# One product of 512 adjacent columns in place of two of 256 in the up projections of two MLPs, with the halves added afterwards

## The reference, cut to what matters

```python
def sq_relu_mlp(h, w1, w2):            # block 1, w1: 1024 x 4096, w2: 4096 x 1024
    return jnp.square(jax.nn.relu(h @ w1)) @ w2
x = x + gt2[..., None, :] * sq_relu_mlp(modulate(rms_norm(x, norm2), sh2, sc2), w_mlp1, w_mlp2)
...
def sqrelu_mlp(xn, w1, w2):            # block 2, the same sizes
    return jnp.square(jax.nn.relu(xn @ w1)) @ w2
h = h + sqrelu_mlp(rmsnorm(h, norm_mlp[i]), mlp_w1[i], mlp_w2[i])
```

## Time and profile before

| | |
|---|---|
| median of three executions | 941.5 us (940.83 to 945.18) |
| the profiled execution: its time | 941.33 us |
| the profiled execution: span from first to last instruction | 939.5 us |
| its mean granted TensorE clock, as a share of full speed | 0.996 |
| instructions | 14931 |
| PE, DVE, ACT busy, of the span | 97%, 66%, 51% |
| matmuls of 256 columns in `product` | 3 x 896 |
| matmuls of 512 columns in `product` | 3 x 592 |

### The profile page before, as it was taken

How to read it: one execution, slowest core, us unless ns; L and a number is a source line. 1 busy time by engine, 2 the same in 40 slices (tenths; PEclk the granted TensorE clock), 3 DMA queues, 4 the chain that set the end, 5 groups by cost and what they waited for, 6 DMA issues and landing times.

```text
span 939.5 us, 14931 instructions
## 1 busy us (share of the span) xinstructions
PE 913.5 (97%) x5552; PEld 789.9 (84%) x5552; DVE 621.5 (66%) x976; ACT 481.8 (51%) x760; POOL 9.7 (1%) x21
## 2 busy tenths in 40 slices
PE   7999999999999999999999999999999999999994
PEld 2778888897789999879999998887888999999883
DVE  1748779769777878765555557655777745555575
ACT  4645455555656565545444444443655544444464
POOL 0200000000000000000000000000000000000000
PEclk9999999999999999999999999999999999999998
DMA  9935212325346767635555557353434765555531
GB/s 361 333 117 201 70 66 90 109 93 176 118 140 220 266 213 259 203 129 185 180 180 181 195 194 261 106 165 128 135 113 146 268 225 179 179 183 194 194 100 45
DMA packets 45347, 162.02 MB, mean 172 GB/s; under 512 B 5616, under 2 KB 5760, under 8 KB 45297
## 3 DMA queue, kind: packets, MB, share of 16 engines
q1 hardware_dynamic: 42896, 155.73, 48.7%
q0 software_dynamic: 1264, 3.89, 1.4%
q10 hardware_dynamic: 1136, 1.70, 0.5%
HBM read 160.25 MB, written 1.05 MB: 172 GB/s over the span
## 4 chain that ended last, share of the span: by engine, by line
PE 83%; DVE 8%; DMA 3%; ACT 3%; issue 1%; SPq 0%; ACTq 0%; DVEq 0%
PE bank L671 71%; DVE w_lo L1613 3%; DMA raw<-in_early 2%; PE bank L828 2%; PE bank L911 1%; DMA arena<-in_early 1%; PE bank L1097 1%; PE bank L818 1%; PE bank L926 1%; PE bank L931 1%; PE bank L835 1%; PE bank L785 1%; DMA raw<-in_stream 1%; ACT w_hi L1194 1%; PE bank L849 1%
## 5 line engine op out<-in xcount | busy, mean ns | idle before, releaser
L1613 DVE TENSOR_TENSOR w_lo<-raw,w_hi 128x1024 fp32r<-128x1024 f32 x246 | 289.8, 1219 | 168.4 <-ACT w_hi L1194 167.9
L1194 ACT ACTIVATE w_hi<-raw 128x1024 fp32r<-128x1024 f32 x246 | 246.1, 1050 | 188.7 <-PE bank L671 169.2
L671 PE MATMUL bank<-act_lo,w_hi 128*128 128x256 f32 x896 | 257.9, 288 | 1.7 <-DVE act_lo L1613 0.9
L671 PE MATMUL bank<-act_hi,w_lo 128*128 128x256 f32 x896 | 253.5, 283 | 0.0
L671 PE MATMUL bank<-act_hi,w_hi 128*128 128x256 f32 x896 | 253.4, 283 | 0.0
L671 PE MATMUL bank<-w_hi,act_lo 128*128 128x512 f32 x592 | 238.5, 403 | 0.0
L671 PE MATMUL bank<-w_hi,act_hi 128*128 128x512 f32 x592 | 231.1, 390 | 0.0
L671 PE MATMUL bank<-w_lo,act_hi 128*128 128x512 f32 x592 | 230.7, 390 | 0.0
L671 PEld LDWEIGHTS bank<-act_lo,w_hi 128*128 128x128 f32 x896 | 171.7, 192 | 5.8 <-DVE act_lo L1613 2.1
L671 PEld LDWEIGHTS bank<-act_hi,w_hi 128*128 128x128 f32 x896 | 171.8, 192 | 1.4 <-issue 0.7
L671 PEld LDWEIGHTS bank<-act_hi,w_lo 128*128 128x128 f32 x896 | 171.7, 192 | 0.0
(11 more groups left out here) (243 smaller groups left out, 785.8 us busy)
## 6 DMA issues: line engine op xcount, KB each, us to landing
raw<-in_stream SPq DMA_DIRECT2D x278, 512.0 KB, 4.4
arena<-in_early SPq DMA_DIRECT2D x12, 512.0 KB, 10.0
raw<-in_early SPq DMA_DIRECT2D x4, 512.0 KB, 15.4
res<-in_x ACTq DMA_DIRECT2D x1, 1024.0 KB, 8.9
arena<-in_ctx SPq DMA_DIRECT2D x1, 1024.0 KB, 14.5
res<-in_x POOLq DMA_DIRECT2D x1, 1024.0 KB, 8.2
arena<-in_norm_final POOLq DMA_DIRECT2D x1, 512.0 KB, 4.4
arena<-in_ple_b POOLq DMA_DIRECT2D x1, 512.0 KB, 5.2
```

The source lines that it names most:

```text
L671: last = pe.matmul(o, left, right, start=start and m == 0, stop=stop and m == 2, skip_group_check=shared)
L1194: return act.activation(o, i, ACT.Copy)
L1613: return dve.tensor_tensor(o, x, hi.bitcast(F32), ALU.subtract)
```

## The change

The activations are laid out as high left, low left, high right, low right, 256 columns each, in one tensor `act`, so that 512 adjacent columns hold an MLP's input as high part and low part. `act_hi` and `act_lo` become views of it, and the right half begins at column `RIGHT` = 512.

An up tile's block and chunk now takes two matmuls in place of three: high weights by the 512 columns (high and low), and low weights by the 256 high columns, added to the left half of the same bank. A block fills a whole bank, and the sum of its two halves is the result. Every tile uses banks 4 to 7, one per block ("b"'s tile 0 uses 4, 5 and two of the banks 0 to 3), so block b of a tile waits until block b of the tile before has been read. ACT copies each block's right half out of PSUM (four of 128 x 256 per tile in place of two relus of 128 x 512); DVE adds the left half (four of 128 x 256 that are new) and then makes the squared relu as max(x, 0) * x in one instruction per two blocks; ACT then writes the rounded copy of that in place of the square. PE's `ada_fin` waits until block 0 of tile 7 has been read.

```diff
+RIGHT = 2 * T
+BLK0 = {"a": 0, "b": 4 * FF_STEPS}
+FIRST_BANKS = {"a": (4, 5, 6, 7), "b": (4, 5, GROUP_AT["wmo0", 0] % 4, GROUP_AT["wmo0", 1] % 4)}
...
-        act_hi = sb("act_hi", [P, KC, 2 * T], F32R)
-        act_lo = sb("act_lo", [P, KC, 2 * T], F32R)
+        act = sb("act", [P, KC, 4 * T], F32R)
+        act_hi, act_lo = act[:, :, 0:3 * T], act[:, :, T:4 * T]
...
+            def up_chunk(bank, ts, k, col):
+
+                cols_ = slice(col, col + P)
+                pe.matmul(bank[:, :], w_hi[:, ts, k, cols_], act[:, k, 0:2 * T], start=(k == 0), stop=False,
+                          skip_group_check=True)
+                return pe.matmul(bank[:, 0:T], w_lo[:, ts, k, cols_], act_hi[:, k, 0:T], start=False, stop=(k == KC - 1),
+                                 skip_group_check=True)
...
@@ first_up
-                    for g in range(2):
-                        for b in range(2):
...
+                    for b in range(4):
+                        if half == 0 and b >= 2:
+                            if tag == "b":
+                                pe.wait_ge(evac_dve, EVAC["wmo0", b - 2][1])
+                            else:
+                                wait_block(pe, name, b)
+                        for k in range(4 * half, 4 * half + 4):
+                            if b == 0 and k % 2 == 0:
+                                wait_cut(pe, UNIT[tag + "u0", k // 2])
+                            last = up_chunk(psum[FIRST_BANKS[tag][b]], ts, k, b * P)
                         if half == 1:
                             last.then_inc(hid_done, 1)
-                        elif g == 0 and tag == "b":
+                        elif b == 1 and tag == "b":
                             turn(name, (2, 3))
@@ up
-                for g in range(2):
-                    if not (isinstance(i, int) and i < 2):
-                        pe.wait_ge(relu_done, 2 * i + (UP0[tag] + g - 3))
...
+                for b in range(4):
+                    pe.wait_ge(add_done, 4 * i + (BLK0[tag] + b - 3))
+                    for k in range(KC):
+                        if b == 0 and k % 2 == 0:
+                            wait_cut(pe, 8 * i + (first + k // 2))
+                        last = up_chunk(psum[4 + b], ts, k, b * P)
                     last.then_inc(hid_done, 1)
@@ mlp of PE
                 if tag == "a":
+                    pe.wait_ge(add_done, BLK0[tag] + 4 * FF_STEPS - 3)
                     ada_fin(psum[4], 11).then_inc(gt_done, 1)
@@ hidden of ACT
+                banks = FIRST_BANKS[tag] if isinstance(i, int) and i == 0 else (4, 5, 6, 7)
+                for b in range(4):
+                    act.wait_ge(hid_done, 4 * i + (BLK0[tag] + b + 1))
+                    if b % 2 == 0 and not (isinstance(i, int) and i == 0 and tag == "a"):
+                        act.wait_ge(hsq_done, 2 * i + (UP0[tag] + b // 2 - 1))
+                    act.activation(hid_r[:, b // 2, b % 2 * T:(b % 2 + 1) * T], psum[banks[b]][:, T:2 * T],
+                                   ACT.Copy).then_inc(cross_done, 1)
                 for g in range(2):
-                    act.activation(hid_r[:, g], psum[4 + 2 * c + g][:, :], ACT.Relu).then_inc(relu_done, 1)
...
-                    act.activation(act_hi[:, 4 * c + 2 * g:4 * c + 2 * g + 2, T:2 * T],
-                                   hid_r[:, g].rearrange("p (b t) -> p b t", b=2), ACT.Square).then_inc(hhi_done, 1)
+                    hi_part(act_hi[:, 4 * c + 2 * g:4 * c + 2 * g + 2, RIGHT:RIGHT + T],
+                            hid_h[:, g].rearrange("p (b t) -> p b t", b=2)).then_inc(hhi_done, 1)
@@ hidden of DVE
                 for g in range(2):
-                    dve.wait_ge(relu_done, 2 * i + (UP0[tag] + g + 1))
-                    dve.tensor_tensor(hid_h[:, g], hid_r[:, g], hid_r[:, g], ALU.mult).then_inc(hsq_done, 1)
+                    for b in (2 * g, 2 * g + 1):
+                        dve.wait_ge(cross_done, 4 * i + (BLK0[tag] + b + 1))
+                        cross = hid_r[:, g, b % 2 * T:(b % 2 + 1) * T]
+                        dve.tensor_tensor(cross, psum[banks[b]][:, 0:T], cross, ALU.add).then_inc(add_done, 1)
+                    dve.wait_ge(add_done, 4 * i + (BLK0[tag] + 2 * g + 2))
+                    dve.scalar_tensor_tensor(out=hid_h[:, g], in0=hid_r[:, g], scalar=0.0, in1=hid_r[:, g], op0=ALU.max,
+                                             op1=ALU.mult).then_inc(hsq_done, 1)
```

More of the change, by code:

```diff
@@ L731, in mm @@
                 elif kind == "lr":
+                    both = act[:, :, :].rearrange("p k (h v t) -> p v k h t", h=2, v=2)
                     for k in range(KC):
-                        last = product(o[0:2 * RANK, :], (lr_w[0][:, k], lr_w[1][:, k]), acts(k), slice(0, 2 * T),
-                                       slice(0, 2 * RANK), k == 0, k == KC - 1, feature_major=True)
+                        last = product(o[0:2 * RANK, :].rearrange("p (h t) -> p h t", h=2), (lr_w[0][:, k], lr_w[1][:, k]),
+                                       (both[:, 0, k], both[:, 1, k]), slice(0, 2), slice(0, 2 * RANK), k == 0,
+                                       k == KC - 1, feature_major=True)
                 elif kind == "p":
@@ L744, in mm @@
                             wait_chunks(k)
-                        last = product(o[:, :], chunk(n, k), acts(k), slice(base + which * P, base + which * P + P),
-                                       slice(0, NC), k == 0, k == KC - 1)
+                        at = base + which * P if which < TT else RIGHT + (which - TT) * P
+                        last = product(o[:, :], chunk(n, k), acts(k), slice(at, at + P), slice(0, NC), k == 0,
+                                       k == KC - 1)
                 elif n in ("gk", "mq"):
@@ L1314, in turn @@
                 i, y = TURN_AT[name], turn_y
-                half = T if name == "n1" else 0
+                half = RIGHT if name == "n1" else 0
                 for b in quarters:
```

53 lines of the change are left out of this document (17 added, 36 removed).

## The result

| | before, same chip | after |
|---|---|---|
| median | 941.37 us (10 runs, 940.76 to 945.18) | 943.51 us (10 runs, 941.59 to 945.02) |
| profiled execution, its span | 941.33, 939.5 us | 942.63, 940.8 us |
| mean granted clock of the profiled execution | 0.996 | 0.995 |

The ratio is 1.0023, with an interval of 1.0014 to 1.0031: 2.1 us slower where 2.0 us faster than the profiled execution was forecast. The time lies inside the predicted range and within 0.5% of before, but on the other side of it.

The account below looks back on a forecast made before the run. The prediction took PE, busy for 97% of the span, to bound the kernel. Gains of 1.8 us in "a" and 0.2 in "b" took 941.33 us to 939.3, with a range of 936.0 to 944.0.

Parts of the forecast that it names:

- The pair: In up tiles, one 512- and one 256-column matmul cost 347 ns, not 360: 0.41 us less per tile.
- Rivals 1: Up tiles: the weight load is hidden wholly, 340 ns a pair, 0.64 us a tile, 936.1 us; chance 0.13.
- Rival 3: Up tiles: the pair gains nothing, costing the 360 ns of three; 4.1 us slower, 945.4 us; chance 0.07.
- Of DMAs nothing is added or moved: Whole kernel: each DMA is issued when its unit is cut, and cuts stay tied to the ends of tiles.
- Loop: Middle tiles: `hidden` takes DVE 2.0 us more, but all new waits cost nothing, with 0.5 to 4 us in hand.
- Start of "a": Up 1 of the first MLP needs tile 0's banks, read by 419.1; PE arrives at 422.3, no wait.
- End of "a": First MLP's end: tile 7's 0.41 us is lost, down 7 starts 2.0 us later and "mq" moves by 1.1.
- Start of "b": Second MLP: up 1 waits for DVE's first add of tile 0; PE idle 3.1 us, up 1 ends 2.0 late.
- End of "b": Second MLP's end: `hidden` ends at 886.5 where PE asks at 886.22, costing 0.3 us.
- Rival 2: At three edges the waits don't come and all 16 tiles count: 6.6 us, 934.7 us; chance 0.06.
- rival 4: The clock falls in the new idle stretch before up 1 of "b": 11.1 us more, 950.4 us; chance 0.08.
- The sum: Whole kernel: 1.8 us gained in "a" and 0.2 in "b", 2.0 in all, giving 939.3 us.

Follow-up runs that it names:

- e2: The changed kernel with each block's long products (512 columns) all before its short ones (256): 942.46 us, ratio 1.0015.
- e8: The changed kernel with the short product added to the right half of the bank instead of the left: 942.0 us, one run.
- e1: The changed kernel with GpSimd's wait before the loads of norm_final and ple_b put back to its old place: 943.57 us, ratio 1.0024.
- e9: The changed kernel with an extra unused max-and-square on DVE, twice per loop tile, 1.2 us together: 944.69 us, ratio 1.0033.
- e11: e6 with down 7's first part waiting for the low parts by halves, its first two chunks needing only the first: 937.34 us, ratio 0.9958.
- e6: The changed kernel with the edits of e1, e2 and e3 together: 938.73 us, ratio 0.9977.
- e12: e11 with one useless matmul behind `ada_fin` at the end of the first MLP: 937.13 us, ratio 0.9956.
- e10: The changed kernel with useless matmuls in both new idle stretches, three before up 1 of "b", two at the end of "a": 942.41 us, ratio 1.0014.
- e3: The changed kernel with up tiles 1 to 7 of the second MLP using banks in the order 6, 7, 4, 5: 939.42 us, ratio 0.9984.
- e4: The changed kernel with six useless fp32 matmuls of 512 columns in front of up 1 of the second MLP: 944.01 us, ratio 1.0039.

## Why the prediction was wrong, step by step

**The pair was mis-sized. This is the step that failed.** "So a pair costs 227 + 120 = 347 ns" took both transitions from the edges of tiles, and both are right there and in e2's first block of eight. In the loop a pair costs 353. That is half the gain: 0.22 us a tile and not 0.41, some 2.5 us less over the 13 tiles that the sum counted. Why the loop has 353 is open: e8 rules out the half of the bank, e2 shows that grouping brings it to 348, and tiles 0 and 1 of "a" in e1 show that the same order can cost 347. The bounds of 340 and 360 held it; my own narrower range of 344 to 352 did not. Rivals 1 and 3 fall with it. (Rival 3's 2.7 us in "b" should have been 2.4, 731.7 + 11.5 against 740.80, and its time 945.1; nothing else hangs on that.)

By an estimate from the gap that the Trainium skill gives (TensorE: Matmul & The Clock Gate, Back-to-back issue gap), a pair takes 325 ns and three products of 256 take 328. e2 shows 226 and 120 where it has 216 and 109, so the forecast was right to go by the rows.

**"Of DMAs nothing is added or moved" was wrong.** I counted the DMAs of SyncE's ring, and not the wait of GpSimd on a semaphore whose count the change doubles. Price, by e1: 0.42 us of stall against the profiled execution of after, but nothing against that of e8, whose loads are as early.

**The waits came where they were forecast, though not all for the reasons given.** Loop: covered, shown by e9. Start of "a": no wait; up 0 itself started 0.36 earlier, outside the change's reach. End of "a": from up 7's start to "mq" 36.37 us became 37.66 (557.36 and 555.64 to the earlier trace rows and 593.30), 1.3 longer where 1.1 was forecast. That is near by luck, since two steps were wrong the opposite way: DVE's cuts for "mq" were to move by 1.1 and moved by 0.59, and "PE's own four parts, two transposes and 11 us fit into that" was false, since DVE waits 0.61 us for PE's third part. e11, where PE starts down 7 earlier, has "mq" 1.0 earlier. Start of "b": idle 3.12 us where 3.1 was forecast; down 0 was to start at 742.8 and started at 742.96. On the scale of the stage, which began 0.39 earlier, that is 0.55 worse: 0.4 by DVE's later cuts, beside the early loads, and 0.1 by up 1's pace. That the idle time agrees to 0.02 us is luck too: on that scale DVE's first add and PE's arrival (729.03, for 728.6 forecast) both came 0.4 late. End of "b": 0.3, as forecast (e11 gets 0.3 back there: from the start of down 6 to the last part of down 7 PE takes 19.86 us, in e6 20.16). Rival 2 falls.

**The clock** was rival 4, with the right mechanism and the wrong size and place. The price put on it was an up tile at half clock, 11.1 us; in e1 it is 2.9 us, since the clock is back before the tile is half through, and in e6 and e9 1.6 and 1.7. It does not fall in every execution, and it falls at a second place, the end of "a", which I did not name. It fell after idle stretches of 2.41 (e6), 2.70 (e1), 2.80 (e2) and 3.37 us (e9), and did not after 2.69 (e8) and 3.12 (after). I held "five idle microseconds lose it" against my 3.1, when the row said only that it had fallen after five. The kernel before is not free of it either: one of its 22 executions beside e9 to e12 has a clock of 0.991 and 945.16 us.

**The sum.** Forecast for the profiled execution -2.0 us, measured +1.3. Of the 3.3 between: 2.5 by the pair, 0.55 at the start of "b", 0.2 at the end of "a", less 0.36 that came from before the MLP; some 0.4 stays, about what down tiles of 10.94 and not 10.91 make (14 x 0.03 = 0.4). From there to the medians, another 0.8 us by which after's lies further from before's, goes with the clock (e10: 0.7 to 1.1).

The range (936.0 to 944.0) and the chances held because the unknown pair and the clock were in them as rivals. "Slower than before by 2 us" was not among the cases: each missing part alone is small, and I had added only forecasts of one sign.

## What to carry to other kernels

A gain per matmul read from one transition is a bound, not a price: look for a stretch that alternates as the new code will, and even then keep the bounds wide, since one order cost 347 here and 353 there. When a change makes a semaphore count in other steps, list every wait on it, on every engine; a wait that is met too early makes no error here, it only lets a DMA out at a bad time. And where a change asks for more PSUM banks, look at the first and last tile of a loop before the middle: two banks swapped (e3) took 3.1 us off the span, some 2.4 of it their own, nearly what the shorter pair brings in the 13 tiles that count (13 x 0.22 = 2.9).

## What the runs showed of the hardware that was not expected

Matmuls of 512 and of 256 moving columns, each with a new stationary operand of 128 x 128, cost 226 and 120 ns in e2's first block of eight, 348 ns a pair over its tile, and in turn 353 ns a pair in the loop (236 for the long one, 116 for the short), whichever half of the bank the short one adds to. But the same order cost 347 in tiles 0 and 1 of "a" in five profiled executions and 353 there in three. PE stood idle for 2.41 (e6), 2.70 (e1), 2.80 (e2) and 3.37 us (e9), and the granted clock fell to 0.50 (1.2 GHz): in e1 and e2 still within the stall and for 6.8 us, at a price of 2.9 us (e1), in e6 and e9 behind it and for 3.4 us, at 1.6 and 1.7. After 2.69 us in e8 and 3.12 us in the profiled execution of after it did not fall. A float32 matmul of `keep_awake`, 512 columns, takes 0.86 us from one to the next in a row of six (e4); it fills a stall quickly, and too many of them are a stall.
